# Router matmuls with the residual blocks stationary, the first expert's rows picked in turned form, and the row copies ahead of the third rounding

## What is computed

```
logits = xt @ w_r                          # 320 x 1024 by 1024 x 8
top_v, top_i = top_k(logits, 2)
w = softmax(top_v)
for e in range(8):
    h = silu(xt @ wg[e]) * (xt @ wu[e])    # 1024 -> 3584
    y += gates[:, e] * (h @ wd[e])         # 3584 -> 1024
```

## Time and profile before

| | us |
|---|---|
| median of three runs | 1546.27 (1544.8 to 1548.24) |
| the profiled execution, its own time | 1544.94 |
| the profiled execution, its span | 1543.1 |
| TensorE busy | 1531.2 (99%) |
| VectorE busy | 1235.1 (80%) |
| ScalarE busy | 998.6 (65%) |
| the expert stage, from the first piece on | from 582.5 to the end |

### The profile page before, as it was taken

The page is one execution under the profiler, slowest core; times in us unless marked ns, Lnnn a source line. Parts: engine busy times, 40 slices in busy tenths (PEclk is TensorE's granted clock), DMA queues, the critical chain, the costliest instruction groups (busy, mean ns, idle before and its releaser), DMA issues.

```text
span 1543.1 us, 21554 instructions
## 1 busy us (share of the span) xinstructions
PE 1531.2 (99%) x8400; PEld 1330.4 (86%) x8400; DVE 1235.1 (80%) x1255; ACT 998.6 (65%) x1079; POOL 219.0 (14%) x249
## 2 busy tenths in 40 slices
PE   9999999999999999999999999999999999999998
PEld 7988999999998877888888888888888888888886
DVE  5867666654577758989888988998898898898897
ACT  5555433333456547777778777777777777777775
POOL 5514400001150414101001002002002002002000
PEclk9999999999999999999999999999999999999999
DMA  7333455444443459999999999999999999999995
GB/s 225 96 110 114 149 164 163 134 154 151 128 119 109 137 195 327 400 374 383 375 369 383 380 368 375 392 364 377 387 368 378 382 365 375 401 358 369 395 368 180
DMA packets 159701, 437.43 MB, mean 283 GB/s; under 512 B 12068, under 2 KB 66176, under 8 KB 145264
## 3 DMA queue, kind: packets, MB, share of 16 engines
q1 hardware_dynamic: 151796, 423.02, 74.5%
q0 software_dynamic: 5552, 9.62, 2.3%
q10 hardware_dynamic: 2252, 3.41, 0.7%
HBM read 429.40 MB, written 13.60 MB: 287 GB/s over the span
## 4 chain that ended last, share of the span: by engine, by line
PE 96%; DVE 2%; ACT 1%; issue 0%; DMA 0%; SPq 0%; DVEq 0%; ACTq 0%
PE bank L1974 33%; PE bank L2455 13%; PE bank L2466 13%; PE bank L2459 13%; PE bank L2477 7%; PE bank L2480 7%; PE bank L2486 7%; PE bank L1977 2%; PE bank L2495 2%; DVE split_lo L1800 1%; DMA gla<-b_g 0%; DVE cut_lo L1338 0%; DVE x L1965 0%; ACT cut_hi L907 0%; ACT split_hi L1201 0%
## 5 line engine op out<-in xcount | busy, mean ns | idle before, releaser
L1800 DVE TENSOR_TENSOR split_lo<-raw,split_hi 128x2048 fp32r<-128x2048 f32 x336 | 762.8, 2289 | 99.8 <-ACT split_hi L1201 98.8
L1201 ACT CAST split_hi<-raw 128x2048 fp32r<-128x2048 f32 x336 | 640.5, 1911 | 223.0 <-PE bank L2466 144.2
L2455 PE MATMUL bank<-split_hi,xgT_hi 128*128 128x512 f32 x896 | 291.3, 395 | 0.2 <-ACT xgT_hi L1248 0.2
L2459 PE MATMUL bank<-split_hi,xgT_lo 128*128 128x512 f32 x892 | 285.5, 390 | 0.0
L2466 PE MATMUL bank<-split_lo,xgT_hi 128*128 128x512 f32 x896 | 239.9, 389 | 0.0
L907 ACT CAST cut_hi<-ring 128x1024 fp32r<-128x1024 f32 x124 | 129.9, 1049 | 169.1 <-PE bank L1974 165.2
L1974 PE MATMUL bank<-xT_hi,cut_hi 128*128 128x320 f32 x752 | 235.3, 313 | 1.0 <-DVE cut_lo L1338 1.0
L1974 PE MATMUL bank<-xT_hi,cut_lo 128*128 128x320 f32 x752 | 232.3, 309 | 0.0
L1974 PE MATMUL bank<-xT_lo,cut_hi 128*128 128x320 f32 x752 | 230.7, 307 | 0.0
L1338 DVE TENSOR_TENSOR cut_lo<-ring,cut_hi 128x1024 fp32r<-128x1024 f32 x124 | 152.8, 1233 | 83.8 <-ACT cut_hi L907 83.2
L2466 PEld LDWEIGHTS bank<-split_lo,xgT_hi 128*128 128x128 f32 x896 | 168.1, 188 | 35.0
(11 more groups left out here) (306 smaller groups left out, 1609.4 us busy)
## 6 DMA issues: line engine op xcount, KB each, us to landing
raw<-moe_w_gate SPq DMA_DIRECT2D x112, 1024.0 KB, 8.1
raw<-moe_w_up SPq DMA_DIRECT2D x112, 1024.0 KB, 8.0
raw<-moe_w_down SPq DMA_DIRECT2D x112, 1024.0 KB, 7.4
ring<-w_in SPq DMA_DIRECT2D x15, 1024.0 KB, 5.5
ring<-ffn_w_gate SPq DMA_DIRECT2D x11, 1024.0 KB, 5.5
ring<-ffn_w_up SPq DMA_DIRECT2D x11, 1024.0 KB, 5.3
ring<-ffn_w_down SPq DMA_DIRECT2D x10, 1024.0 KB, 5.0
ring<-w_out SPq DMA_DIRECT2D x8, 1024.0 KB, 5.0
```

Of the source, the lines that this page charges most:

```text
L1201: return nc.scalar.copy(split_hi[:, i % SR, :], raw_piece(i)).then_inc(hi_ready, 1)
L1800: V.tensor_tensor(split_lo[:, i % SR, :], raw_piece(i), split_hi[:, i % SR, :].bitcast(F32), ALU.subtract).then_inc(lo_ready, 1)
L2455: TE.matmul(o, xgT_hi[:, kk, :], hi[:, w * k + 512 * c:w * k + 512 * c + 512], start=kk == 0, stop=False)
L2459: TE.matmul(o, xgT_lo[:, kk, :], hi[:, w * k + 512 * c:w * k + 512 * c + 512], start=False, stop=False)
```

## The change

Three edits:

1. `logits` now has the residual block stationary and `wr` moving: for each of the eight feature blocks three matmuls, one for each token tile, in the order 0, 2, 1, each with 8 moving columns. The result stands in bank 7 as tokens by 8 at once. `lgT`, its copy and the three transposes (job `lgr`) are gone; `lgs` is copied straight from `lg`.
2. The pick now has the 128 x 128 blocks of `x` stationary and `Gown` moving (128 columns): 24 matmuls that give the picked rows already turned, straight into banks 4 and 5. The two copies to `xg`, the eight transposes and the semaphores `x0_full`, `x0_left`, `x0_right` are gone. The wait for `RT.free` (the count has been read) now stands behind the pick.
3. On ScalarE `first_hi(2)` stands behind the three copies `x_copy(RC, ...)` instead of ahead of them; `row_squares(1)` follows `row_squares(0)` at once, and `row_squares(2)` stands between the two halves of `xgT_hi`.

```diff
-JOBS["D"] += [("lg",), ("lgr",), ("own",)]
+JOBS["D"] += [("lg",), ("own",)]
...
             x_copy(RS, 2, 0)
-            first_hi(2)
             act.wait_ge(RC.free, RC.emptied(("wo", 1, WO_RING.rindex("C"))))
             x_copy(RC, 0, 1)
             x_copy(RC, 1, 1)
             x_copy(RC, 2, 1)
+            first_hi(2)
             row_squares(0)
+            row_squares(1)
...
-            act.wait_ge(x0_full, 1)
-            nc.scalar.copy(xg[:, 0:512], banks[2][:]).then_inc(x0_left, 1)
-            row_squares(1)
             xg_hi(0, 0, range(4))
+            row_squares(2)
             xg_hi(0, 0, range(4, KB))
-            row_squares(2)
...
             dve.wait_ge(RD.full, RD.filled(("lg",)))
-            V.tensor_copy(lgT[:], RD.bank(("lg",))[0:NE, 0:T]).then_inc(RD.free, 1)
-            dve.wait_ge(RD.full, RD.filled(("lgr",)))
             for t, (t0, rows) in enumerate(TILES):
-                last = V.tensor_copy(lgs[0:rows, t], RD.bank(("lgr",))[0:rows, NE * t:NE * t + NE])
+                last = V.tensor_copy(lgs[0:rows, t], RD.bank(("lg",))[0:rows, NE * t:NE * t + NE])
...
             first_lo(1)
             first_lo(2)
-            dve.wait_ge(x0_full, 2)
-            V.tensor_copy(xg[:, 512:1024], banks[3][:]).then_inc(x0_right, 1)
             xg_lo(0, 0)
...
                     pe.wait_ge(R.free, R.emptied(job))
-                    last = mm(RD.bank(("lg",))[0:NE, 0:T], wr[:, k, :], xR[:, k, :], k == 0, k == KB - 1)
+                    for t in (0, 2, 1):
+                        t0, rows = TILES[t]
+                        last = mm(RD.bank(("lg",))[0:rows, NE * t:NE * t + NE], xR[:, k, t0:t0 + rows], wr[:, k, :], k == 0 and t == 0, k == KB - 1 and t == 1)
...
             x_rows(RS, 2, 0)
-            b = RD.begin(pe, ("lgr",))
-            for t, (t0, rows) in enumerate(TILES):
-                last = tr(b[0:rows, NE * t:NE * t + NE], lgT[:, t0:t0 + rows], NE)
-            last.then_inc(RD.full, 1)
             x_rows(RC, 0, 1)
...
             pe.wait_ge(G_ready, 1)
             pe.wait_ge(RS.free, RS.count)
             pe.wait_ge(RC.free, RC.count)
+            for half in range(2):
+                for k in range(4):
+                    for t, (t0, rows) in enumerate(TILES):
+                        last = mm(tb[half][:, P * k:P * k + P], x[0:rows, t, 512 * half + P * k:512 * half + P * k + P], Gown[0:rows, t, :], t == 0, t == NT - 1)
+                last.then_inc(t_full, 1)
             pe.wait_ge(RT.free, RT.count)
-            for half in range(2):
-                for t, (t0, rows) in enumerate(TILES):
-                    if half and t == NT - 1:
-                        xg_T(0, None, [0])
-                    last = mm(banks[2 + half][:], Gown[0:rows, t, :], x[0:rows, t, 512 * half:512 * half + 512], t == 0, t == NT - 1)
-                last.then_inc(x0_full, 1)
...
-                        if first and i == 0:
-                            xg_T(0, None, [1])
                         pe.wait_ge(lo_ready, ip * (2 * NP) + (i + 1 + PR))
```

More of the change, by code:

```diff
@@ L414, in build @@
         front.close()
-        token_rows = ExitStack()
-        lgT = sb("lgT", [NE, T], F32, token_rows)
-        token_rows.close()
         hmT_hi = sb("hmT_hi", [P, FEB, P], FR)
@@ L497, in build @@
         G_ready, own_ready, tags_ready, idx_ready, pairs_ready = sem("G_ready"), sem("own_ready"), sem("tags_ready"), sem("idx_ready"), sem("pairs_ready")
-        lgT_ready, x0_full, x0_left, x0_right, table_zero, table_out, table_in = sem("lgT_ready"), sem("x0_full"), sem("x0_left"), sem("x0_right"), sem("table_zero"), sem("table_out"), sem("table_in")
+        table_zero, table_out, table_in = sem("table_zero"), sem("table_out"), sem("table_in")
         idc_ready, isc_ready, xg_in, rows_out, masks_ready, now_ready = sem("idc_ready"), sem("isc_ready"), sem("xg_in"), sem("rows_out"), sem("masks_ready"), sem("now_ready")
@@ L1831, in _ @@
             dve.wait_ge(RD.full, RD.filled(("lg",)))
-            V.tensor_copy(lgT[:], RD.bank(("lg",))[0:NE, 0:T]).then_inc(RD.free, 1)
-            dve.wait_ge(RD.full, RD.filled(("lgr",)))
             for t, (t0, rows) in enumerate(TILES):
-                last = V.tensor_copy(lgs[0:rows, t], RD.bank(("lgr",))[0:rows, NE * t:NE * t + NE])
+                last = V.tensor_copy(lgs[0:rows, t], RD.bank(("lg",))[0:rows, NE * t:NE * t + NE])
             last.then_inc(RD.free, 1)
-            dve.wait_ge(RD.free, RD.emptied(("lgr",)))
+            dve.wait_ge(RD.free, RD.emptied(("lg",)))
             for t in range(NT):
@@ L2394, in _, with xg_T @@
             tb = [banks[4], banks[5]]
[L2396 to L2402, removed]
+            def xg_T(first, base):
+                for i in range(2):
+                    pe.wait_ge(t_free, base + (first + i - 1))
                     for k in range(4):
```

## The result

The changed kernel takes 1552.73 us (median of 22 runs, 1549.07 to 1564.63) against 1545.44 us before (22 runs, 1544.22 to 1548.53). The ratio is 1.0053, 95% interval 1.004 to 1.0066: slower by 0.53%, or 7 to 8 us. I had forecast 1548.4, with 1550.3 as the upper end. The spread grew too, from 4 us to 15 us.

What follows compares the result with a forecast made beforehand. TensorE was taken to bound the kernel: first piece 2.6 us later, 0.5 won in it, so the second piece 2.1 later; on 1544.94 that gives 1547.0, and 1548.4 for the median, 1.3 higher. Range 1543.8 to 1550.3.

Steps and rivals of the forecast that it cites:

- What bounds the kernel: Expert stage: runs at TensorE's pace, so a us won or lost ahead of it moves the end by a us.
- What a small f32 matmul costs: Router and pick on TensorE: 0.11 us a 128-column record, about 0.10 per width change, 0.20 per row-count change.
- Edit 2: Pick: 24 matmuls in eight rounds of 1.07, 8.55 us; first piece can begin 2.6 us later than before.
- the 0.5 of the first piece: Expert stage's first piece: takes 2.73 us and not 3.23, so 0.5 won.
- Edit 3: ScalarE's order of rounding, row copies and square sums: costed at nothing.
- Edit 1: Router: eight rounds of 0.75, 6.0 us in all; lgs starts 0.8 us later.
- the rivals: Router and pick: free shape changes (1543.5, chance 0.17), no overlap of short matmuls (1553.6, 0.08), a wash (1546.3, 0.17).
- The second of them: Rival for router and pick: short matmuls with new stationary operands don't overlap, +7.3 us, 1553.6; chance 0.08.

Runs made afterwards that it cites:

- changed_fourth: The changed kernel run once more with a profile, no edit: 1561.38 us.
- old_router: Changed kernel with the router edit undone (eight matmuls of 320 columns, lgT copy and transposes back), pick and ScalarE order kept: 1547.8 us, ratio 1.001 to the kernel before.
- router_64col: Changed kernel with wr's 8 columns moved eight times over (64 moving columns) in each router matmul: 1549.14 us, ratio 1.0021 to the kernel before.
- router_only: The router edit alone on the kernel before, with the old pick and ScalarE order: 1551.02 us, ratio 1.0028.
- both_grouped_8col: Changed kernel with pick and router matmuls grouped by token tile, 8 moving columns in the router: 1547.37 us, ratio 1.001 to the kernel before.
- router_wide: Changed kernel with wr's 8 columns moved sixteen times over (128 moving columns) in each router matmul: 1550.65 us, ratio 1.0022 to the kernel before.
- order_only: Kernel before with only first_hi(2) moved behind ScalarE's three row copies: 1546.64 us, ratio 1.0004.
- changed_fifth: The changed kernel run once more with a profile, no edit: 1564.52 us.

## Why the prediction was wrong

- **What bounds the kernel** held. The expert stage passes a shift on one to one: the second piece begins 7.6 later than in the kernel before and the span is 7.7 longer; in changed_fourth it is 16.3 and 16.5.
- **What a small f32 matmul costs** held at full clock: 0.75 a router round (0.76 measured), 1.07 a pick round (1.06), the pick 8.4 us in old_router, where I had 8.55.
- **Edit 2** held: old_router shifts by +1.2 at full clock, which is my 2.6 less the 0.8 that was edit 1's and the 0.5 of the first piece, to 0.1.
- **Edit 3** held, at nothing, as far as it was run by itself (the rounding).
- **Edit 1 is the step that failed**, in the sentence "Eight are 6.0. The last matmul begins at 566.19 + 6.0". It prices all 48 records at 0.75 a round, at the clock of the window that I had quoted, 1.00 in the expert stage, without asking whether the new router would keep it. It took 8.4 us, `lgs` came 3.0 later behind the router's start and not 0.8, and behind it ranks, filler and pick ran at half clock. None of the rivals had this, and no chance was given to a lower clock. The second of them had the right sign, the right place and nearly the right time (1553.6), but another mechanism, loads that don't overlap, and that one is refuted by the 0.11 of every round at full clock.
- The clue was in the shapes. The old router moved 320 columns for each 8 loaded; the new one moves 8 for each 128. The page counts a weight load as work (PEld), and the records of the 8-column matmuls last 0.26 (the one at 567.30) where they begin 0.11 apart, so they overlap and TensorE looked busy for 100% of the stretch.
- The Trainium skill (TensorE: Matmul & The Clock Gate, "What's actually happening" in the part on the clock gate) says that the low clock is the default and that activity releases it. The trace agrees, in the direction that I had left out: an engine with no gap in its instructions lost its clock, and of two routers with the same instructions the one that did more work kept it. By that rule router_64col could be faster than the changed kernel, with more work and not less; it was, by 3.6 us, or by 4.3 if each is taken against the kernel before in its own comparison.
- The time is above the range because the range was made of the bounds of one clock only, and the width of the spread (15 us) was not in it at all.

## What to carry to other kernels

When operands are swapped so that a narrow matrix moves and a wide one is loaded, price the new form at full clock and then ask what the array itself does in that stretch: read the granted clock of every window behind it, not the busy share. If the clock falls, make the moving operand wider with a repeated access before giving the form up. Repeated to 64 columns it made the router 6.9 us long for the 6.0 that I had for 8 columns at full clock; repeated to 128 it was 8.2. And group short matmuls by the shape of their stationary operand: leaving and entering a tile of another row count cost 0.2 us each time.

## What the runs showed of the hardware

- With 8 moving columns for each load of 128, the granted clock fell from 1.00 to 0.50 between 2.7 and 5.5 us behind the router's start in all seven profiled executions that had such a router (five of the changed kernel, router_only, both_grouped_8col); with 64 or 128 columns and the same loads it did not in any of three. How long it stays low differs between executions of one kernel, in the changed kernel from about 7 to 31 us. That makes 10 of its spread of 15 us (shifts of +4.7 to +14.8); the rest is the low clock at the start, below.
- Changes of the stationary shape cost 0.1 us (width, behind a matmul of 8 columns) and 0.2 us (row count) each.
- Executions of several kernels have a low clock between 11 and 21 us from the start (in the profiled executions of old_router, router_only, router_wide, router_64col, order_only, changed_fourth and changed_fifth), and what follows begins 1.5 to 5 us later. The profiled execution of the kernel before has none; that others of its executions have is concluded from their mean clock. Windows of order_only, where the low clock stood there in the profiled execution (the other windows had 1.00):

```profile
12.00:16.00 4.00, 4.00 (x17) 2.14 (x16) 3.82 (x8) 3.91 (x8) 0.00 (x0) 0.62 1.14 295
16.00:20.00 4.00, 4.00 (x16) 4.00 (x17) 3.12 (x6) 3.94 (x8) 0.00 (x0) 0.53 0.84 260
```

  The times of the kernel before go with its mean clock in the same way: about 1544.7 at 1.00, 1546 to 1547 at 0.998, 1548 to 1549 at 0.996 and 1550.8 at 0.995. What decides in which executions this happens stays open, and so does what decides whether the low clock behind the router ends before the pick or behind it.
